# Reordering the attention of layer 0 and the delta-rule groups of layer 1 in a two-layer decoder kernel

## What is computed

```python
for i in range(DEPTH):                       # 2
    mem_kv = mem @ mem_w_kv[i]
    if i % 2 == 0:
        h = x @ mla_w_in[j]
        mix = mla_mixer(h[..., :MLA_MIX_IN], cos, sin, ...)   # 12 causal heads
    else:
        h = x @ gdn_w_in[j]
        mix = gdn_mixer(h[..., :GDN_MIX_IN], ...)             # conv, chunked delta rule
    mem_o = memory_attention(h[..., -MEM_WIDTH:], mem_kv)     # 4 heads, not causal
    y = jnp.concatenate([mix, mem_o], -1) @ w_out[i]
    x = layer_norm(ALPHA * x + y, ln1_g[i], ln1_b[i])
    ff = jnp.square(jax.nn.relu(x @ mlp_w1[i])) @ mlp_w2[i]
    x = layer_norm(ALPHA * x + ff, ln2_g[i], ln2_b[i])
```

## Time and profile before

| what | us |
| --- | --- |
| median of three executions | 2470.22 |
| their range | 2469.14 to 2471.08 |
| the profiled execution | 2471.89 |
| its span, first to last instruction | 2470.1 |

### The profile page before, as it was taken

How to read it: one execution, slowest core, us unless ns; L and a number is a source line. 1 busy time by engine, 2 the same in 40 slices (tenths; PEclk the granted TensorE clock), 3 DMA queues, 4 the chain that set the end, 5 groups by cost and what they waited for, 6 DMA issues and landing times.

```text
span 2470.1 us, 35483 instructions
## 1 busy us (share of the span) xinstructions
PE 2384.2 (97%) x13572; PEld 2078.7 (84%) x13577; DVE 1467.5 (59%) x1550; ACT 1071.8 (43%) x1340; POOL 247.9 (10%) x221
## 2 busy tenths in 40 slices
PE   8999989999999999999999999989899999999997
PEld 7897778888888888889899898978788888888885
DVE  6654567546555556577756757545865554555555
ACT  4455444434444444354535435333443443443443
POOL 0150001001000001000122320310010000000000
PEclk9999999999999999999999999999999999999999
DMA  6662456565566565655424324126455665656654
GB/s 233 188 187 94 137 172 200 199 193 188 192 185 196 192 191 182 200 190 162 137 69 139 108 79 154 60 90 226 140 188 195 184 196 196 187 190 195 188 191 158
DMA packets 234624, 417.10 MB, mean 169 GB/s; under 512 B 23761, under 2 KB 42474, under 8 KB 232938
## 3 DMA queue, kind: packets, MB, share of 16 engines
q1 hardware_dynamic: 233114, 410.73, 52.2%
q10 hardware_dynamic: 1360, 4.19, 0.4%
HBM read 412.77 MB, written 2.10 MB: 168 GB/s over the span
## 4 chain that ended last, share of the span: by engine, by line
PE 48%; issue 40%; DVE 5%; POOL 4%; ACT 2%; DMA 1%; SPq 0%; POOLq 0%; ACTq 0%; DVEq 0%
PE quad L563 10%; PE quad L592 6%; PE quad L590 6%; PE quad L591 6%; PE quad L566 5%; PE quad L534 3%; PE quad L536 3%; PE quad L538 3%; DVE cv L1793 2%; POOL hl L2070 1%; ACT whi L1036 1%; PE quad L947 1%; PE quad L934 1%; DVE wlo L1413 1%; PE quad L944 1%
## 5 line engine op out<-in xcount | busy, mean ns | idle before, releaser
L1413 DVE TENSOR_TENSOR wlo<-raw,whi 128x1024 fp32r<-128x1024 f32 x760 | 979.1, 1297 | 726.1 <-ACT whi L1036 724.0
L1036 ACT ACTIVATE whi<-raw 128x1024 fp32r<-128x1024 f32 x760 | 798.7, 1058 | 979.7 <-PE quad L592 525.8
L563 PE MATMUL quad<-xs,whi 128*128 128x512 f32 x2048 | 649.9, 397 | 7.4 <-DVE xs L1673 3.7
L590 PE MATMUL quad<-whi,hh 128*128 128x512 f32 x1344 | 528.9, 393 | 5.2 <-DVE hl L1548 3.7
L592 PE MATMUL quad<-whi,hl 128*128 128x512 f32 x1344 | 523.8, 390 | 0.0
L591 PE MATMUL quad<-wlo,hh 128*128 128x512 f32 x1344 | 523.5, 390 | 0.0
L566 PEld LDWEIGHTS quad<-xs,wlo 128*128 128x128 f32 x2048 | 386.7, 189 | 91.0
L566 PE MATMUL quad<-xs,wlo 128*128 128x256 f32 x2048 | 403.8, 279 | 0.0
L563 PEld LDWEIGHTS quad<-xs,whi 128*128 128x128 f32 x2048 | 314.6, 190 | 10.0 <-DVE wlo L1413 5.5
L590 PEld LDWEIGHTS quad<-whi,hh 128*128 128x128 f32 x1344 | 252.7, 188 | 60.0 <-issue 7.2
L592 PEld LDWEIGHTS quad<-whi,hl 128*128 128x128 f32 x1344 | 252.5, 188 | 53.1
(11 more groups left out here) (286 smaller groups left out, 2103.4 us busy)
## 6 DMA issues: line engine op xcount, KB each, us to landing
raw<-in_mlp_w SPq DMA_DIRECT2D x512, 512.0 KB
raw<-in_gdn_w_in SPq DMA_DIRECT2D x105, 512.0 KB
raw<-in_w_out SPq DMA_DIRECT2D x64, 512.0 KB
raw<-in_mem_w_kv SPq DMA_DIRECT2D x32, 512.0 KB
raw<-in_mla_w_in SPq DMA_DIRECT2D x25, 512.0 KB
raw<-in_mla_w_ukv SPq DMA_DIRECT2D x24, 256.0 KB
gb<-in_ln_g SPq DMA_DIRECT2D x4, 1024.0 KB, 6.5
gb<-in_ln_b SPq DMA_DIRECT2D x4, 1024.0 KB, 8.5
```

What stands on the lines that cost most here:

```text
L563: last = nc.tensor.matmul(both, b.whi[:, slot, k, cols], b.xs[:, :, kt, :], start=start, stop=stop, skip_group_check=True)
L590: nc.tensor.matmul(ps[:, t, 0:n], ah[:, kt, toks], hi[:, k, 0:n], start=start, stop=False)
L1036: nc.scalar.activation(b.whi[:, c % NSPLIT], b.raw[:, slot], ACT.Copy).then_inc(sem.hi_ready, 1)
L1413: nc.vector.tensor_tensor(b.wlo[:, c % NSPLIT], b.raw[:, c % NRAW], b.whi[:, c % NSPLIT].bitcast(F32), ALU.subtract).then_inc(sem.lo_ready, 1)
```

## The change

1. **Layer 0.** The memory heads are heads 0 to 3 of the pipeline, the causal heads 4 to 15. The pipeline starts right after the turns of ckv, and the latent panels stand inside its first seven steps (`LATENT_STEPS`): two panels in each of steps 0 to 3, one v panel in each of steps 4 to 6. The output chunks stand in steps 7 to 18, those of the memory heads first (`OUT0_ORDER`, which SP's loads follow), four more behind the loop. The three groups of rotated turns come after steps 2, 6 and 9 (`ROTATED_STEPS`), each behind a wait for the copy of the probabilities that lie in the same bank.
2. **Delta-rule groups.** On ACT `kbt` is copied ahead of the tanh. `vn` is copied straight from PSUM ahead of `uu`, and the waits for `d_u` stand later. `conv(g + 1, 0)` moves from behind the turned rows of group g to ahead of them, with the scaling of the rows inside it, and PE takes four chunks of k instead of three before it turns the rows. `conv(g, 1)` has a split inside it on both engines.
3. **Last group.** Its rows are scaled in step 0 of the memory heads' pipeline and turned in step 2, into the banks of the panel qm1; output chunks 4 and up wait for them.

The diff, cut to its core:

```diff
+LATENT_STEPS = {0: [("qrope", 0), ("qrope", 1)], 1: [("qnope", 0), ("qnope", 1)], 2: [("qnope", 2), ("knope", 0)],
+                3: [("knope", 1), ("knope", 2)], 4: [("v", 0)], 5: [("v", 1)], 6: [("v", 2)]}
+OUT0_ORDER = list(range(NH // CK, PANEL)) + list(range(NH // CK))
+ROTATED_STEPS = [2, 6, 9]
...
+            pe.wait_ge(sem.turn_f, TURN_AT["ln1_0"])
...
+            def rotated_step(i):
+
+                if i in ROTATED_STEPS:
+                    g = ROTATED_STEPS.index(i)
+                    pe.wait_ge(sem.pt_out, i - 1)
+                    turn_rotated(g)
...
+            attention(0, mem_heads + [dict(causal=True, q=b.qn[:, h, :], k=b.kn[:, h, :], rope=(h % 2, h // 2),
+                                           ready=PANEL_AT["v"], v_ready=PANEL_AT["v"] + h // 4 + 1,
+                                           v=lambda kb, h=h: b.vrows[:, kb, h * P:(h + 1) * P]) for h in range(NH)],
+                      latent_step, rotated_step)
...
                 for t in tiles:
                     pe.wait_ge(sem.a_w, n0 + t + 1)
-                    pe.wait_ge(sem.d_u, n0 + t + 1)
...
-                if g < HG - 1:
-                    turned_panel(f"k{g + 1}", 0, 3)
+                if g == HG - 1:
+                    return
+                turned_panel(f"k{g + 1}", 0, 4)
+                turn_rows(g, turn_ps)
...
                     for t in range(TT):
                         act.wait_ge(sem.p_kt, n0 + t + 1)
                         bank_out(b.kt, t, turn_ps, sem.a_kt)
+                    for t in range(TT):
+                        act.wait_ge(sem.p_kbt, n0 + t + 1)
+                        bank_out(b.kbt, t, side_ps, sem.a_kbt)
 
                 conv(g, 2, keys_out)
-                for t in range(TT):
-                    act.wait_ge(sem.p_kbt, n0 + t + 1)
-                    bank_out(b.kbt, t, side_ps, sem.a_kbt)
...
+                dve.wait_ge(sem.p_u, n0 + 1)
+                nc.vector.tensor_copy(b.vn[0:CHUNK, 0].rearrange("p h c -> p (h c)"),
+                                      side_ps[0][0:CHUNK, :]).then_inc(sem.d_vn, 1)
...
+                if g == HG - 1:
+                    return scaled, turned_out
+                conv(g + 1, 0, 1, scaled)
+                feed(1)
+                turned_out([turn_ps[(TURN_AT[f"gdn{g}"] + k) % 2] for k in range(2)])
```

More of the change, by code:

```diff
@@ L622, in short_rows, with turn @@
                 last.then_inc(then, 1)
-            def turn(g, src, kts):
+            def turn(g, src, kts, bank=None):
+                ps = turn_ps[g % 2] if bank is None else bank
                 if g >= 2:
@@ L684, in _, with latent_panel, turn_rotated @@
             last.then_inc(sem.rot_t, 1)
[L685 to L699, removed]
+            def latent_panel(name, i):
+                p, c = PANEL_AT[name] + i, CHUNK_AT[name] + 2 * i
+                if name == "qrope":
+                    panel_r(p, c, 2, b.ch, b.cl, after_turn("cq"), n=6 * ROPE)
+                elif name == "qnope":
+                    panel_t(p, c, 2, b.ch, b.cl, after_turn("cq"))
+                elif name == "knope":
+                    panel_t(p, c, 2, b.ch[:, 4:8, :], b.cl[:, 4:8, :], after_turn("ckv"))
+                else:
+                    panel_r(p, c, 2, b.ch[:, 4:8, :], b.cl[:, 4:8, :], after_turn("ckv"))
+            def turn_rotated(g):
+                pe.wait_ge(sem.rot_done, 3)
                 for i in range(2):
@@ L727, in key_blocks @@
             def key_blocks(n):
-                return [(kb, t) for kb in range(TT) for t in range(TT) if n >= NH or t >= kb]
+                return [(kb, t) for kb in range(TT) for t in range(TT) if not NM <= n < NM + NH or t >= kb]
             def turn_probs(n):
@@ L750, in values, with attention @@
                 last.then_inc(sem.o_done, 1)
-            def attention(n0, heads, between):
+            def attention(n0, heads, between, after=lambda i: None):
                 n = len(heads)
@@ L757, in attention @@
                     if i < n:
+                        if heads[i]["ready"] is not None:
+                            pe.wait_ge(sem.panel_free, heads[i]["ready"])
                         scores(n0 + i, heads[i]["causal"], heads[i]["q"], heads[i]["k"], heads[i]["rope"])
@@ L781, in _ @@
             mem_heads = [dict(causal=False, q=b.qm[:, h, :], k=b.km[:, h, :], rope=None,
+                              ready=PANEL_AT["qm0"] + 1, v_ready=None,
                               v=lambda kb, h=h: b.vm[:, kb, h * P:(h + 1) * P]) for h in range(NM)]
-            attention(0, [dict(causal=True, q=b.qn[:, h, :], k=b.kn[:, h, :], rope=(h % 2, h // 2),
-                               v=lambda kb, h=h: b.vrows[:, kb, h * P:(h + 1) * P]) for h in range(NH)] + mem_heads,
-                      lambda i: out0_chunk(i - 5) if i >= 5 else None)
@@ L1167, in head_hi, with attention @@
                 act.wait_ge(sem.o_done, n + 1)
[L1168 to L1170 removed]
+                nc.scalar.activation(b.hh[:, head_tile(n % KT), :], o_ps[:, 0:S], ACT.Copy).then_inc(sem.o_hi, 1)
+            def attention(n0, n, fed_from, fed_steps, at=lambda i: None, after=lambda i: None):
                 for i in range(n0, n0 + n + 3):
+                    at(i - n0)
                     if n0 <= i - 2 < n0 + n:
@@ L1391, in _, with rows_hi @@
             take_t("qm1", 0, b.qm, 0, scale_mem)
-            attention(NH + NM, NM, 0, NH // CK)
+            def rows_hi(i):
+                if i == 3:
+                    for k in range(2):
+                        split_turn(TURN_AT[f"gdn{HG - 1}"] + k, b.hh, (HG - 1) * GH + 2 * k)
+            attention(NH + NM, NM, 0, NH // CK, rows_hi)
             feed(UP * PANEL - NH // CK)
@@ L1782, in _, with conv @@
                                   turn_ps[1][:, 0:NC * NH]).then_inc(sem.gcum_set, 1)
-            def conv(g, i, splits=0):
+            def conv(g, i, splits=0, between=lambda: None):
                 m = 3 * g + i
@@ L1936, in _, with rows_step @@
                 conv(g, 2, 2)
-                gdn(g)
-            attention(NH + NM, NM, 0, NH // CK)
+                last_group = gdn(g)
+            def rows_step(i):
+                scaled, turned_out = last_group
+                if i == 0:
+                    scaled()
+                if i == 2:
+                    turned_out([panel_ps[PANEL_AT["qm1"] % 2][:, (TURN_AT[f"gdn{HG - 1}"] + k) % 2, :] for k in range(2)])
+            attention(NH + NM, NM, 0, NH // CK, rows_step)
             feed(PANEL - 1 - NH // CK)
```

191 lines of the change are left out of this document (123 added, 68 removed).

## The result

The changed kernel takes 2440.08 us (median of four executions, 2437.57 to 2443.05); the kernel before, beside it on the same chip, 2470.65 (2469.14 to 2472.87). The ratio is 0.9876, 95% interval 0.9859 to 0.9893: 1.2% faster. The prediction said 2440.5, between 2433 and 2452.

A forecast was written before the change was run, and what follows sets the result against it. TensorE, busy 97% of the span, was taken to set the time. Layer 0 4.6, delta-rule groups 4.4, 7.0 and 9.8, last group 9.0, less 5.1 for clock, gave 29.7 off 2470.2: 2440.5 us, range 2433 to 2452.

The forecast's parts named there:

- (a): Layer 0, start of the heads: head 0's scores wait for DVE's copies behind a split, a new stall of 2.9 us.
- (b): Layer 0, step 2: rotated turns wait for the probabilities' copy behind ACT's latent-panel work, a new stall of 2.4 us.
- (c): Layer 0, step 4: head 4's scores wait for the last knope panel, a new stall of 1.2 us.
- (d): Layer 0, step 6: rotated turns wait behind ACT's panel work, values cover 0.7; a new stall of 1.8 us.
- (e): Layer 0, step 9: rotated turns with no panel ahead of them, a new stall of 0.2 us.
- (f): Delta-rule groups: kbt ahead of the tanh removes 3.6 us of waits and 1.7 of clock, 0.9 back; net 4.4.
- (g): Delta-rule groups: vn straight from PSUM removes three waits, 3.6 us, and 3.4 of low clock; net 7.0.
- (h): Group boundaries: the next q's earlier convolution removes 5.3 us of waits, 3.0 of clock, 1.5 for wlo; net 9.8.
- (i): Last group: waits of 6.0 and 3.3 us and 3.1 of clock go, 3.4 of new waits come; net 9.0.
- the clock doesn't follow: Rival: no new low-clock stretch, 2435; or four new stalls cost 3.4 us or more, vn's stay, 2446; chance 0.25.
- the group's boundary: Rival at the delta-rule group boundary: PE waits for a split or or_set, (h) fails, 2445 to 2450; chance 0.12.
- the circle of ACT and PE: Rival in layer 0: ACT's work circles with PE's turns, 2 us more in all 19 steps, 2479; chance 0.03.

The follow-up runs named there:

- l0_pure: Kernel before with only the rearrangement of layer 0's heads, every delta-rule edit undone; 2468.1 us, ratio 0.9991.
- u_kbt: Changed kernel with the copy of kbt put back behind the tanh; 2441.3 us, ratio 0.9890.
- u_split: Changed kernel with the split inside the convolution of k put back behind it; 2442.6 us, ratio 0.9894.
- u_vn: Changed kernel with vn copied from uu again and PE waiting for uu first, as before; 2444.8 us, ratio 0.9902.
- u_conv: Changed kernel with the next group's first convolution and PE's fourth chunk of k put back behind the turned rows; 2446.3 us, ratio 0.9901.
- u_rows: Changed kernel with the last group's rows scaled, turned and rounded ahead of the memory heads, as before; 2444.0 us, ratio 0.9893.
- f_b: Changed kernel with layer 0's rotated turns moved one step later, inside the step; 2434.9 us, ratio 0.9854.
- f_a: Changed kernel with head 0's scores in layer 0 issued behind the first latent panel; 2434.6 us, ratio 0.9854.
- f_all: Changed kernel with head 0's and head 4's scores and rotated turns later, qm1's copy ahead of ACT's split, last group's rounding a step earlier; 2426.6 us, ratio 0.9822.
- l0_only: Kernel before with layer 0's change, plus the changed place of the split inside the convolution of k; 2459.2 us, ratio 0.9951.

## Why the prediction was right

**What bounds the kernel** held: DVE has 4.5 us more of busy time than before, and the kernel is 32 us faster. In the thirteen profiles with the new layer 0, the span less PE's waits and its clock is the same to 2 us.

**Layer 0, what comes.** (a) was 2.9 and is 2.99, (b) 2.4 and 2.23, (c) 1.2 and 0.9 to 1.1, (d) 1.8 and 1.37, (e) 0.2 and at most 0.2. They were right since ACT and DVE do in after what the earlier trace rows showed, in the same order: ACT's list behind a latent panel in after reads

```profile
178.65 1.06 ACT L1113 ACTIVATE whi<-raw 128x1024 fp32r<-128x1024 f32 x1 [1.76 <-PE quad L553]
179.61 1.07 ACT L1141 ACTIVATE kn<-quad 128x512 f32<-128x512 f32 x2
180.57 0.60 ACT L1240 ACTIVATE probt<-quad 128x512 f32<-128x512 f32 x1
```

and PE starts at 181.22, when the last is done. **What goes.** The waits of the chunks for `hl` and the rotated turns' own are gone, and the loss that shows no idle row, reckoned at 2.6 (1.5 + 1.1), is in the balance as the remainder's 4.6 at most. The layer's end came 2.4 us earlier in the first profile of after, with two stretches at the low clock, and 3.8 earlier in the second, with one. The prediction had 4.6 before the clock, so 1.2 with two stretches and 2.9 with one. On its own (l0_pure) the layer gives 0.0009 of the ratio, 2.2 us, by the interval 0.2 to 4.4. So the mechanism held and its net was some 1 us off, within what is measured. The 0.3 us that each restart was to cost stands in no row.

**(f)** was right in its number and wrong in part of its cause. The waits for `kbt` went, and by the times u_kbt prices the copy at 4.6 us against 4.4, with an interval as wide as that; its waits grow by only 1.9. But a part was booked under it that the split's place had done, and this split stood at nothing in the sum. The step that failed is that the split's new place was taken as the same work in another place, without asking which load and which chain it lets start earlier. The 0.9 us back didn't come, for the same reason: in group 0 DVE ends the scaling by the decay at 1213.33, 4.7 us earlier than in the earlier trace rows, and PE, some 3.3 us earlier than reckoned, turns that q at 1213.77, 0.4 us behind it. In u_split it waits 0.7 there.

**(g)** 7.0, and u_vn gives 7.5. **(h)** 9.8: u_conv gives 7.3 for the convolution, and the waits for `wlo` counted in it (1.5) turned out to be the split's: u_conv doesn't have them, u_split and l0_pure do. The slack was smaller than said. k6, the first chunk that DVE splits behind its copies of the turned rows, was ready in time with nothing to spare, where 1 us had been reckoned: DVE ends its split at 1315.33, and PE passes to that chunk at 1315.42. DVE's splits and POOL's instructions there:

```profile
1313.37 1.96 DVE L1511 TENSOR_TENSOR wlo<-raw,whi 128x1024 fp32r<-128x1024 f32 x1 [1.65 <-ACT whi L1113]
...
1315.25 2.06 DVE L1511 TENSOR_TENSOR wlo<-raw,whi 128x1024 fp32r<-128x1024 f32 x1
...
1311.68 2.56 POOL L2113 TENSOR_TENSOR hl<-xf,hh 128x512 fp32r<-128x512 f32 x2 [9.59 <-ACT hh L1134]
...
1314.20 2.03 POOL L2203 TENSOR_TENSOR nt<-tri,glog 128x512 f32<-128x512 f32 x1
```

The two splits take 0.74 and 0.84 us more than a split alone (1.22 in after); the prediction had 0.7 and read it as less than a full block. That reading was wrong. POOL's instructions in progress end at 1314.24 and 1316.23, 0.87 and 0.98 us behind the start of the splits, and each split ends 1.1 us behind that. So each did its work when POOL's instruction was over, and was late by what was left of it, not by its whole length of 1.3. The longest splits of this trace, 3.42 us at 383.16 among them, show it best: POOL's instruction beside that one ends 2.34 us behind its start, and the split 1.08 behind that. The Trainium skill's page "SBUF — State Buffer", section "Who interferes with whom", says that DVE with two SBUF inputs and a reading GpSimd instruction block each other fully, and the trace agrees. The 1 to 2 us that the prediction drew from the page didn't come, since no split started together with POOL's instruction and k6 had just enough slack.

**(i)** 9.0, net of 3.4 for the new waits (2.4 and 1.0; measured 2.36 and 1.26). u_rows gives 5.3 by the times. Its profile has 5.7 in waits and 2.7 of the clock, against the 3.1 reckoned: 8.4. The two differ by less than the intervals, and the runs don't tell which is nearer.

**The clock.** Three new stretches were counted, at 1.7 each. The first profile has two, the second one, f_b one and f_a none. The rival "the clock doesn't follow" (2435) thus took part of the place of the forecast. By the balance the low clock costs 10.4 us less than before. The terms had 6.1, or 8.6 with the part that stood in the 6.8 of the rotated turns, and one stretch too many on the other side.

**The sum.** 29.7 us were forecast. Against the mean ratio it is 31.7; the single parts, each undone, are 9.8 (f and split), 7.5 (g), 7.3 (h), 5.3 (i) and 2.2 (layer 0, by itself), together 32.1. So the parts add, as far as intervals of some 5 us on each can show. The total fits better than its parts, and that is luck. The split, worth some 5 us, was left out. (h), (i) and layer 0 were set 2.5, 3.7 and 2.4 us too high by these times, which hold their shares of the clock, and the 5.1 us for new stretches at the low clock made up for part of that. None of the rivals of a failing mechanism came: not the group's boundary (no wait for `wlo` there), not layer 0's loss, not the circle of ACT and PE, which f_all rules out with waits of 1.0 us in all of layer 0's attention.

## What to carry to other kernels

Where one engine is busy 97% of the span, list its waits, give each edit the rows it removes and the rows it makes, and price a made wait by following the releasing engine's list in the rows of the same instructions elsewhere: here all such prices were within 0.5 us. Give every moved instruction its term, even one split that stays in its phase; by PE's waits the only edit booked at nothing was worth at least as much as the one it stood beside. Price a split beside POOL by what is left of POOL's instruction when it starts. After the result, balance the span against waits and half the busy time at the low clock: a remainder that differs between two kernels is a loss that shows no idle row.

## What the runs showed of the chip

The same wait in the same program isn't always followed by the low clock. The wait of 2.99 us ahead of the first scores stands in eleven of the profiles; in six of them a stretch at the low clock follows, in five not. The window behind it reads 0.50 in after (the row at 143.90 above) and 1.00 in u_split:

```profile
143.50:146.90 3.40, 3.40 (x20) 3.30 (x20) 0.69 (x1) 1.33 (x4) 2.12 (x2) 1.00 0.40 117
...
179.20:182.60 3.40, 3.34 (x12) 2.98 (x13) 0.48 (x1) 1.52 (x6) 2.82 (x9) 0.50 0.59 168
```

The second row stands behind the wait of 2.23 us, where the clock fell, and the same wait in f_a left it at full:

```profile
176.50:179.90 3.40, 3.40 (x28) 3.30 (x27) 1.69 (x4) 1.12 (x5) 2.85 (x9) 1.00 0.56 156
```

Of the three waits of 1.2 us for `vn`, one was followed by 3.4 us at the low clock in u_vn, and two in the kernel before. A single profile thus over- or understates a wait by 1.7 us, and executions of one kernel differ by 2 to 9 us. Where they differ most it is in step with the mean clock: of l0_only's five, that with 0.987 took 2464.6 and those with 0.990 2456.5 and 2456.6. From before to after a microsecond of PE's waits went with 1.6 us of time (20.0 us of waits in the two stretches, 31.7 of time), from there to f_all with 1.2 (9.9 and 12.2). Over the kernels with one part undone it is 0.9 to 2.4, with the intervals said above.
